# Block 1's pre-norms: the norm weight moved out of the first product, and three of the eight products moved from VectorE to GpSimd

## The reference, cut to what matters

```python
def rmsnorm(x, g):
    xf = x.astype(jnp.float32)
    y = xf * lax.rsqrt(jnp.mean(xf * xf, axis=-1, keepdims=True) + RMS_EPS)
    return (y * g.astype(jnp.float32)).astype(x.dtype)

for l in range(DEPTH):                       # DEPTH = 2
    h = rmsnorm(x, norm_mix_pre[l])          # pre-norm 1
    ... = split_cols(h @ w_in[l], IN_SPLITS)
...
    h = rmsnorm(x, norm_mem_pre[l])          # pre-norm 2
    x = x + rmsnorm(memory_cross_attention(h, mem_n, ...), norm_mem_post[l])
    h = rmsnorm(x, norm_ffn_pre[l])          # pre-norm 3
    u = h @ w_up[l]
```

## Time and profile before

| | |
|---|---|
| median of 3 runs | 4299.95 us (4299.09 to 4310.45) |
| profiled execution: span of the trace | 4308.8 us |
| profiled execution: its own device time | 4310.55 us |
| PE / DVE / ACT / POOL busy, share of the span | 90% / 51% / 39% / 1% |
| mean granted TensorE clock | 0.925 |

### The profile page before, as it was taken

The page is one execution under the profiler, slowest core; times in us unless marked ns, Lnnn a source line. Parts: engine busy times, 40 slices in busy tenths (PEclk is TensorE's granted clock), DMA queues, the critical chain, the costliest instruction groups (busy, mean ns, idle before and its releaser), DMA issues.

```text
span 4308.8 us, 52229 instructions
## 1 busy us (share of the span) xinstructions
PE 3881.4 (90%) x18218; PEld 3154.0 (73%) x18218; DVE 2204.6 (51%) x3735; ACT 1664.4 (39%) x2458; POOL 53.3 (1%) x104
## 2 busy tenths in 40 slices
PE   7999979998999988999797867799998888788997
PEld 5888857876878866877586656688887766676885
DVE  4634557777643456778345553523333446545333
ACT  3333444323233354332536654412222346553222
POOL 0000000000000000001000000000000000000000
PEclk9999989998999999999897757999999987789999
DMA  3212313454221322446115000111111110112222
GB/s 120 89 59 88 111 55 117 145 177 135 97 71 58 107 93 78 144 143 214 47 59 51 0 0 15 39 64 64 61 60 49 64 35 0 26 41 69 93 93 73
DMA packets 117857, 334.51 MB, mean 78 GB/s; under 512 B 38127, under 2 KB 38895, under 8 KB 117103
## 3 DMA queue, kind: packets, MB, share of 16 engines
q1 hardware_dynamic: 83087, 269.06, 20.1%
q0 software_dynamic: 14400, 52.44, 3.9%
q10 hardware_dynamic: 20256, 11.53, 1.0%
HBM read 330.89 MB, written 6.97 MB: 78 GB/s over the span
## 4 chain that ended last, share of the span: by engine, by line
PE 78%; DVE 10%; ACT 5%; issue 3%; DVEq 2%; DMA 1%; ACTq 1%; SPq 0%
PE PS L376 12%; PE PS L377 12%; PE PS L378 12%; PE PS L726 10%; PE PS L729 10%; PE PS L727 10%; PE PS L783 3%; PE PS L763 2%; PE PS L757 2%; PE PS L426 2%; PE PS L514 2%; DVE PB L1484 1%; DVE PTL L2005 1%; PE PS L523 1%; ACT PTH L1275 1%
## 5 line engine op out<-in xcount | busy, mean ns | idle before, releaser
L1494 DVE TENSOR_TENSOR WL<-RAW,WH 128x1024 fp32r<-128x1024 f32 x494 | 604.5, 1224 | 544.4 <-ACT WH L937 540.7
L937 ACT ACTIVATE WH<-RAW 128x1024 fp32r<-128x1024 f32 x494 | 521.3, 1055 | 686.6 <-PE PS L729 371.2
L376 PE MATMUL PS<-HHI,WH 128*128 128x512 f32 x1632 | 655.6, 402 | 41.9 <-DVE HLO L1531 36.8
L377 PE MATMUL PS<-HLO,WH 128*128 128x512 f32 x1632 | 646.8, 396 | 0.0
L378 PE MATMUL PS<-HHI,WL 128*128 128x512 f32 x1632 | 641.4, 393 | 0.0
L726 PE MATMUL PS<-H2HI,WH 128*128 128x512 f32 x1472 | 531.2, 361 | 46.6 <-DVE H2LO L1944 35.3
L727 PE MATMUL PS<-H2LO,WH 128*128 128x512 f32 x1472 | 501.1, 356 | 0.0
L729 PE MATMUL PS<-H2HI,WL 128*128 128x512 f32 x1472 | 436.0, 356 | 0.0
L376 PEld LDWEIGHTS PS<-HHI,WH 128*128 128x128 f32 x1632 | 309.5, 190 | 134.4 <-issue 47.1
L726 PEld LDWEIGHTS PS<-H2HI,WH 128*128 128x128 f32 x1472 | 280.1, 190 | 126.2 <-issue 40.9
L378 PEld LDWEIGHTS PS<-HHI,WL 128*128 128x128 f32 x1632 | 309.8, 190 | 70.2
(11 more groups left out here) (281 smaller groups left out, 6404.9 us busy)
## 6 DMA issues: line engine op xcount, KB each, us to landing
RAW<-in_stream SPq DMA_DIRECT2D x494, 512.0 KB, 3.3
MODW<-in_modw POOLq DMA_DIRECT2D x96, 512.0 KB, 4.1
bias_rows<-in_rpb SPq DMA_DIRECT2D x1, 4762.5 KB, 54.2
BIAS<-bias_rows ACTq DMA_DIRECT2D x20, 224.0 KB, 3.9
MEM<-in_mem ACTq DMA_DIRECT2D x3, 1024.0 KB, 4.8
X<-in_x SPq DMA_DIRECT2D x1, 2048.0 KB, 9.1
CROW<-in_crow POOLq DMA_DIRECT2D x4, 512.0 KB, 4.8
out<-X SPq DMA_DIRECT2D x1, 2048.0 KB, 7.4
```

The lines of the kernel that those rows point to most:

```text
L376: nc.tensor.matmul(out, WH[:, slot, b * P:(b + 1) * P], hi, start=start, stop=False)
L377: nc.tensor.matmul(out, WH[:, slot, b * P:(b + 1) * P], lo, start=False, stop=False)
L937: A(WH[:, d, :], RAW[:, s, :], ACT.Copy).then_inc(high_split, 1)
L1494: TT(WL[:, d, :], RAW[:, s, :], WH[:, d, :].bitcast(F32), ALU.subtract).then_inc(split_ready, 1)
```

## The change

The weight leaves the first product, so that this becomes X times root, a tensor_tensor. It is applied twice later: ScalarE's high part becomes an Identity activation whose scale is the weight's column, and VectorE's low part becomes a scalar_tensor_tensor, value times weight minus high part. Three of the eight products X times root (blocks 2, 4 and 6) are made by GpSimd, which starts on a semaphore that VectorE raises as its norm begins. ScalarE waits for GpSimd's semaphore at these three blocks. VectorE has 13 instructions in place of 16 in each pre-norm, ScalarE 8 as before, and GpSimd 3.

```diff
+POOL_ROOTED = (2, 4, 6)
...
+        rooted_from, pool_rooted = sem("rooted_from"), sem("pool_rooted")
...
             for l in range(DEPTH):
 
+                def rooted(norm):
+
+                    pool.wait_ge(rooted_from, 3 * l + norm + 1)
+                    for k in POOL_ROOTED:
+                        nc.gpsimd.tensor_tensor(HVAL[:, k, :], X[:, k, :], RS[:, 0:T], ALU.mult).then_inc(pool_rooted, 1)
+
+                rooted(0)
                 before_up = (l + 1) * UNITS_1 - DOWN_UNITS * KB - 2 * FF
...
                     pool.dma_start(CROW[v][:], crow[v * D:(v + 1) * D].partition_broadcast(P)).then_inc(crow_in, 16)
+                rooted(1)
+                rooted(2)
                 pool.wait_ge(units_done, before_up + 1)
...
-            def norm_high(n=T):
+            def norm_high(norm, gain):
                 for k in range(KB):
-                    high(HHI[:, k, :], HVAL[:, k, 0:n])
+                    if k in POOL_ROOTED:
+                        act.wait_ge(pool_rooted, norm * len(POOL_ROOTED) + POOL_ROOTED.index(k) + 1)
+                    else:
+                        m.add("val")
+                        act.wait_ge(val_ready, m.at("val"))
+                    A(HHI[:, k, :], HVAL[:, k, :], ACT.Identity, scale=PL[:, gain + k:gain + k + 1]).then_inc(hi_ready, 1)
...
             def norm_apply(gain):
 
-                dve.drain()
+                dve.drain().then_inc(rooted_from, 1)
                 for k in range(KB + 1):
-                    if k < KB:
-                        STT(HVAL[:, k, :], X[:, k, :], par(gain + k), RS[:, 0:T], ALU.mult, ALU.mult).then_inc(val_ready, 1)
+                    if k < KB and k not in POOL_ROOTED:
+                        TT(HVAL[:, k, :], X[:, k, :], RS[:, 0:T], ALU.mult).then_inc(val_ready, 1)
                     if k:
-                        low(HLO[:, k - 1, :], HVAL[:, k - 1, :], HHI[:, k - 1, :])
+                        b = k - 1
+                        m.add("hi")
+                        dve.wait_ge(hi_ready, m.at("hi"))
+                        STT(HLO[:, b, :], HVAL[:, b, :], par(gain + b), HHI[:, b, :].bitcast(F32), ALU.mult, ALU.subtract).then_inc(lo_ready, 1)
```

More of the change, by code:

```diff
@@ L1046, in _ @@
                 act.dma_start(POOLW[:], poolw[l, :, :, :]).then_inc(pool_in, 16)
-                norm_high()
+                norm_high(3 * l + 0, G_MIX)
                 for c in range(2):
@@ L1147, in _ @@
                 root(T)
-                norm_high()
+                norm_high(3 * l + 1, G_MEM)
                 for c in range(HEADS):
@@ L1178, in _ @@
                 root(T, summed=True)
-                norm_high()
+                norm_high(3 * l + 2, G_FFN)
                 act.preload_act_table(ACT.Silu)
```

## The result

| | before | changed |
|---|---|---|
| median of 12 runs each, us | 4309.89 (4299.09 to 4315.87) | 4319.61 (4308.13 to 4328.50) |
| ratio, 95% interval | | 1.0027 (1.0014 to 1.0039) |
| profiled execution: span, granted clock | 4308.8, 0.925 | 4306.3, 0.928 |

The change makes the kernel slower by 0.27% (0.14 to 0.39%), which is 11.6 us on 4309.89; the two medians lie 9.7 us apart. The interval leaves out no change, and the effect is within the 0.3% that the prediction held for too small to tell. The forecast was an increase of 11.3 us on 4299.95, 0.26%. The difference came out, but the time, 4319.61, lies just above the range's end of 4319, because the kernel before is at 4309.89 over twelve runs and not at the 4299.95 of the first three.

What follows compares the result with a forecast made beforehand. VectorE was taken to bound the six pre-norms. Each would take 9.26 + 3 x 1.07 + 0.24 - 0.32 = 12.39 us, 1.88 more; six make 11.3, so 4299.95 + 11.3 = 4311 us, range 4291 to 4319.

Steps and rivals of the forecast that it cites:

- the last of the sum: Whole kernel: the 11.3 us for six pre-norms added to the three-run median of 4299.95, giving 4311 us.
- One for one: Six pre-norms: whatever VectorE gains or loses there reaches the kernel's end in full, TensorE having no slack behind them.
- Exclusion: Pre-norms: VectorE instructions with two SBUF inputs and GpSimd passes reading SBUF alternate; 11.3 us more with passes near 1.07, chance 0.42.
- GpSimd's pass: Each of three products per pre-norm on GpSimd: 1.07 us, bounded by 0.68 and 1.37, stopping VectorE for that length.
- (b): Pre-norms: VectorE and GpSimd exclude each other with a long pass, 12.9 us or more from 1.16 us on; chance 0.26.
- The stretch: Each pre-norm, first value to end of last low part: 12.39 us, 1.88 more than before.
- VectorE's turns: VectorE's instructions in a pre-norm: five values of 0.60 and eight low parts of 0.66 us, 8.28 us back to back.
- the waits of 0.19: Blocks 3, 5 and 7 of each pre-norm: VectorE's low part waits 0.19 us each for ScalarE's longer high part.
- Holds and handovers: Each pre-norm: three GpSimd passes stop VectorE 1.07 us each, plus 0.08 us per handover, 0.24 together.
- (c): Pre-norms: GpSimd runs freely beside VectorE; 9.26 us each, 7.5 us less in all, 4292.5 us; chance 0.25.
- (d): Pre-norms: VectorE and GpSimd share reads without full exclusion, giving the 7.5 us about back, 4300 us; chance 0.07.
- The chances: Whole kernel's time: slower by over 0.3% had 0.33, faster 0.03, the rest 0.64.

Runs made afterwards that it cites:

- the run with blocks 3, 5 and 7: Changed kernel with root and VectorE's values in PSUM, GpSimd making blocks 3, 5 and 7 in place of 2, 4 and 6: 4297.78 us, 0.9982.
- side products: Kernel before, plus three unused X times X products on GpSimd beside each unchanged pre-norm: 4330.67 us, 1.0050.
- fills: Kernel before, plus three GpSimd passes beside each pre-norm that write zeros and read no tensor: 4312.34 us, 1.0003.
- copies: Kernel before, plus three GpSimd passes beside each pre-norm that each copy one block of X, reading one tensor: 4317.94 us, 1.0022.
- the PSUM runs: Changed kernel with root and VectorE's values in PSUM; GpSimd on blocks 2, 4 and 6: 4300.99 us, 0.9979; on 3, 5 and 7: 4297.78 us, 0.9982.

## Why the prediction was right and where it was wrong

**The step that failed** is the last of the sum, where it was put on a level: "All terms are short waits that do not depend on that, so they go onto the median: 4299.95 + 11.3 = 4311." That the terms do not depend on the level held; the level did not. The three runs were 4310.45, 4299.09 and 4299.95. Twelve, these three among them, give a median of 4309.89, and the two that set the first median are the two lowest of the twelve: an unlucky draw. Two later sets of 29 give 4312.26 and 4310.22. On the level of the twelve the sum is 4309.89 + 11.3 = 4321.2, 1.6 us from the 4319.61 measured. The profile's own 4310.55, which the prediction set aside as near the slowest of three, was the typical one. The range, 4291 to 4319, was built from the rivals' costs alone and left out the spread of the runs, which is as large as the effect: the changed kernel's twelve runs go from 4308.13 at a granted clock of 0.928 to 4328.50 at 0.922.

**One for one.** "So what VectorE gains or loses there goes into the end one for one" holds in sum (10.1 us in the six stretches, 11.6 by the ratio with 6 to 17 in its interval) and not for each pre-norm: between pre-norms 2 and 3 of layer 0 the clock gave 1.5 us back, and in the run with blocks 3, 5 and 7 the first take followed VectorE no further. That 11.3 and 11.6 lie so close is in part luck, since the stretches by themselves cost 10.1.

**Exclusion** held, and the order was alternate as forecast. Each pre-norm has three holds of 1.0 to 1.1 us. They fall on VectorE's second to fourth instruction where its first value starts ahead of GpSimd (stretches of 12.15), and on the first three where GpSimd's first pass does (12.23 and 12.25). The side products, fills and copies show that it takes a GpSimd pass that reads SBUF, and the PSUM runs show that it takes a VectorE instruction with two SBUF inputs. By the rule of the Trainium skill that the prediction weighed (SBUF — State Buffer, Who interferes with whom) a pass that only writes does not contend with such an instruction; the trace with fills agrees (752 ns at most).

**GpSimd's pass** was taken as 1.07 us and holds VectorE for 1.03. That agreement is luck: the 1.07 is the length of a VectorE instruction that reads PSUM (BLO<-PS,BHI in the earlier trace rows), and GpSimd's pass is longer. Undisturbed it has a record of 1.26 to 1.29 us, and three follow each other in 3.73 (the PSUM run). With 1.26 for g the prediction's sum would have been 2.45 us a pre-norm, 14.7 in all, and rival (b), which began at 1.16. What the prediction had as one number is two: the pass, and the hold, which is 0.2 us shorter. A record in the changed kernel is up to 1.82 because it includes the wait for VectorE. The Trainium skill's 4497 ns for 2048 columns (GPSIMD Engine Reference, Performance versus the Vector engine) gave an estimate of 1.12; the undisturbed record of 1.26 is above it and the hold of 1.03 below it, and these decide.

**The stretch** was forecast at 12.39 us and is 12.15 to 12.25; six were to cost 11.3 us and cost 10.1. VectorE's turns, the Identity of 0.72, the low part of 0.75 and the waits of 0.19 for blocks 3, 5 and 7 (1.62 in place of 1.41 for each pair of low parts) came out. Holds and handovers were put at 3 x 1.07 + 0.24 = 3.45 us; VectorE's turns are longer by 3.1 to 3.2 in all, so next to nothing is left for handovers.

**The rivals.** The long pass (b) is out with a hold of 1.03, though the pass itself is long. No exclusion (c) did not happen, but its price did: with the reads apart the stretch is 9.19 us with GpSimd on blocks 3, 5 and 7 (9.30 to 9.63 on 2, 4 and 6), where (c) said 9.26; the shorter high parts from PSUM help a little. Shared reads (d) are out with 12.15 against 10.51. TensorE's added waiting sits at the first block of each pre-norm (7.12 us in place of 5.18). Its waits for these low parts are up from 36.8 to 49.0 us; the 47.7 of the earlier trace rows also counts waits for other tiles that L1531 makes.

**The chances** went with the result: within 0.3% had 0.64.

## What to carry to other kernels

In this kernel work moved to GpSimd was not free, because VectorE's instructions read two tensors from SBUF: each GpSimd pass that reads SBUF stopped VectorE, so moving 0.60 us off VectorE put 1.03 us of standstill on it. With one of VectorE's two operands in PSUM the same three passes run beside it, and the kernel gains 0.2%. Where an effect is of the size of the run-to-run spread, forecast the ratio or the length of the stretch, and take the level from many runs; three can sit 10 us away from twelve.

## What the runs showed of the hardware that was not expected

A GpSimd pass holds VectorE for less time than its own record lasts. A product of 128x512 that meets no wait of its own has a record of 1.26 us and holds VectorE for 1.0 to 1.1; a copy has 0.61 and holds it for 0.37 to 0.40. In both the hold is some 0.2 us shorter than the record; a fill of 0.52, which reads nothing, holds nothing. The held low part 2 of the PSUM run says the same: it ends 0.55 us behind the third pass, and 0.75 is its undisturbed length, so it was let go some 0.2 us before that pass's record ends. What GpSimd does in these 0.2 us no run shows. Most records of products and copies beside VectorE are longer than that (medians of 1715 and 1068 ns), since they include GpSimd's own wait; so the price of a pass is to be read from one that met nothing, or from what it does to the other engine.
